# Token-major products that read their tokens as every second place, and residual rows that hold two neighbouring tokens a partition

## The chip, the cores and the metric

One Trainium2 chip, of which the kernel uses one core. The metric is device time in microseconds (us) of one execution: three runs of the kernel before gave 1893.33, 1895.21 and 1895.46 us, median 1895.21. Everything is fp32: a large product is made as three products of fp32r operands (high parts by high parts, high by low, low by high).

## The reference

Two blocks are applied to 256 tokens of width 2048. The second one also sees 16 meta tokens.

```python
# first block
h = x
h = h + mixer_block(rms_norm(h, norm_mix_w[l]), w_in[l], ...)   # ends in: merged @ w_out
u = rms_norm(h, norm_mlp_w[l])
h = h + jnp.square(jax.nn.relu(u @ w_up[l])) @ w_down[l]        # 2048 -> 8192 -> 2048
x = rms_norm(h, norm_final_w)
# second block
h = jnp.concatenate([meta, x], axis=1)
proj = rmsnorm(h, pre_norm_g) @ w_in_2                          # then two kinds of attention: ya, yb
y = jnp.concatenate([ya, yb], axis=-1) @ w_out_2
h = h + rmsnorm(y, post_norm_g)
return h[:, N_META:, :]
```

## The kernel before

**Weights.** All weights stream through a ring of four slots, in chunks of 256 rows by 512 columns (512 KB). SyncE (SP) issues the transfer into `raw`, ScalarE (ACT) rounds it into `whi`, VectorE (DVE) makes the rest `wlo = raw - whi`, and TensorE (PE) multiplies. A chunk holds two tiles of 128 rows of the contraction (`CK = 2`). Eight chunks (`NC`) make a group, which yields 512 columns of a product.

**Two forms of product.** `chunk_t` takes the weights as the stationary operand and streams the 256 tokens past them: 24 matmuls of 128x256 a chunk, and the result has features on the partitions. `chunk_n` (the natural product) takes 128 tokens as the stationary operand and streams the 512 weight columns: 12 matmuls of 128x512 a chunk, and the result has tokens on the partitions. Its stationary operand is `v[:, kt, toks]`, a run of 128 neighbouring fp32 places in a tile that holds features on the partitions and 256 tokens along each of them; `t` is 0 or 1 for the two halves of the tokens.

**Where the natural product is used.** In the first projection for groups 4, 5, 12 and 13 (`natural`), and in the three stages that add to the residual: `w_out` of the first block (4 groups), `w_down` (4 quarters of 4 groups) and `w_out_2` (4 groups). The residual `h` is a tile of 128 partitions by 2 rows (t) by 2048. It is loaded from `x` by one transfer (line 395) once the attention scores of the first block are issued, and first used when the first group of `w_out` is added to it. The result leaves in five stores (line 423) at the end.

**Turning the rows.** `turn_group` (line 476) transposes 4 feature tiles of both rows of `h` on PE with the identity, 8 transposes a call, into one PSUM tile `turned` of 256 tokens: places 0 to 127 for t = 0 and 128 to 255 for t = 1. It is called four times after `w_out` and four times after the last `w_down`. Line 853 multiplies a matrix of ones by the diagonal of the row scales, which puts the 256 scales along the free axis in the same order (two matmuls).

**Order.** The order of the work on each engine is written out by hand, and the engines meet on semaphores. PE's order is: the first projection (22 groups, with the matmuls of the chunked scan and of attention put between chunks), the branch products, `w_out`, four quarters of `w_up` and `w_down`, the second projection (13 groups, with the second block's attention between chunks), `w_out_2`. In the scan, `level_scores` (line 548) has k_both as its stationary operand and reads `qp` for its moving operand in runs of 1, 2, 4, ... 64 neighbouring elements at levels 1 to 7, from two places in turn.

Of the kernel before, what the change touches and what calls it, by code (L numbers as in the profile page):

```python
# [15 lines left out]
P = 128  # L16
D = 2048
T = 256
NT = T // P
# [15 lines left out]
CK = 2  # L35
NC = KT // CK
# [75 lines left out]
def program(nc, x, w_in, lb_logits, hg_norm_w, rel_bias, w_branch_a, w_branch_b, w_out, norm_mix_w,  # L112
# [3 lines left out]
    with ExitStack() as ctx:  # L116
# [18 lines left out]
        ones = sb("ones", [P, P])  # L135
# [221 lines left out]
        def turned(n, i):  # L357

            o = (i % 2) * T
            return ps[:, 4 + 2 * (n % 2) + i // 2, o:o + T]  # L360
# [4 lines left out]
        @block.sync  # L365
        def _(sp):
            def chunk(c0, k, src):

                if not isinstance(c0, int) or c0 + k >= SLOTS:
                    sp.wait_ge(wlo_ready, c0 + k - SLOTS + 1)  # L370
                    sp.sem_inc(sp_turn, 1)
                sp.dma_start(raw[:, k % SLOTS], src).then_inc(raw_in[k % SLOTS], 16)

            def rows(w, k, cols):
                return w[:, CK * k:CK * k + CK, cols]

            sp.dma_start(ident[:], identity).then_inc(ident_in, 16)
            sp.dma_start(mix_rows[:], norm_mix_w[0].rearrange("(k p) -> k p", p=P)).then_inc(mix_in, 16)
            for c in range(4):
                cols = slice(c * CW, (c + 1) * CW)  # L380
                sp.dma_start(x_nat[:, :, cols], x[0, :, cols].rearrange("(t p) d -> p t d", p=P)).then_inc(x_in[c], 16)
                if c == 0:
                    first = rows(w_in_t, 0, slice(0, CW))
                    sp.dma_start(raw[:, 0, 0], first[:, 0]).then_inc(half_in, 16)
                    sp.dma_start(raw[:, 0, 1], first[:, 1]).then_inc(raw_in[0], 16)
                else:
                    chunk(C_IN, c, rows(w_in_t, c, slice(0, CW)))
            for k in range(4, NC):
                chunk(C_IN, k, rows(w_in_t, k, slice(0, CW)))
            with sp.Fori(1, G_IN) as g:  # L390
                for k in range(NC):
                    chunk(C_IN + NC * g, k, rows(w_in_t, k, bass.ds(g * CW, CW)))

            sp.wait_ge(at_s, AH)
            sp.dma_start(h[:], x[0].rearrange("(t p) d -> p t d", p=P)).then_inc(h_in, 16)
            with sp.Fori(0, 4) as n:
                for k in range(NC):
                    w = w_a_t if k < NC // 2 else w_b_t
                    chunk(C_BR + NC * n, k, rows(w, k % (NC // 2), bass.ds(n * CW, CW)))
            with sp.Fori(0, 4) as n:  # L400
                for k in range(NC):
                    chunk(C_OUT + NC * n, k, rows(w_out_t, k, bass.ds(n * CW, CW)))
            with sp.Fori(0, QUARTERS) as q:
                with sp.Fori(0, 4) as n:
                    for k in range(NC):
                        chunk(C_FF + 8 * NC * q + NC * n, k, rows(w_up_t, k, bass.ds(q * D + n * CW, CW)))
                with sp.Fori(0, 4) as n:
                    for k in range(NC):
                        chunk(C_FF + 8 * NC * q + 4 * NC + NC * n, k,
                              w_down_t[:, bass.ds(q * KT + CK * k, CK), bass.ds(n * CW, CW)])  # L410
            for j, col in enumerate(IN2_COLS):
                for k in range(NC):
                    chunk(C_IN2 + NC * j, k, rows(w_in2_t, k, slice(col, col + CW)))
            with sp.Fori(0, 4) as n:
                for k in range(NC):

                    chunk(C_OUT2 + NC * n, k, rows(w_out2_t, (k + NC // 2) % NC, bass.ds(n * CW, CW)))
            i = 0
            for t in range(NT):
                for lo, hi in OUT_COLS[t]:  # L420
                    i += 1
                    sp.wait_ge(y_out, i)
                    sp.dma_start(out[0, t * P:(t + 1) * P, lo:hi], y2[:, t, lo:hi]).then_inc(stored, 16)
            sp.wait_ge(stored, 16 * i)


# [1 line left out]
        def _(pe):  # L428
# [18 lines left out]
                                     stop=last and j == CK - 1 and i == 2, skip_group_check=True)  # L447
                ins.then_inc(pe_done, 1)

            def chunk_n(c0, k, kt0, xh, xl, s, first, last, halves=range(NT)):  # L450

                pe.wait_ge(wlo_ready, c0 + k + 1)
                for j in range(CK):
                    kt = kt0 + j
                    for t in halves:
                        toks = slice(t * P, (t + 1) * P)
                        for i, (v, w) in enumerate(((xh, whi), (xh, wlo), (xl, whi))):
                            ins = mm(ps[:, 2 * s + t, :], v[:, kt, toks], w[:, k % SLOTS, j, :],  # L458
                                     start=first and j == 0 and i == 0,
                                     stop=last and j == CK - 1 and i == 2, skip_group_check=True)  # L460
                if NT - 1 in halves:
                    ins.then_inc(pe_done, 1)
                return ins
# [4 lines left out]
            def turn_group(b, n, freed):  # L468

                pe.wait_ge(set_free[n % 2], freed)  # L470
                if n >= 2:
                    pe.wait_ge(x_ready, KT * b + 4 * n - 4)
                for i in range(4):
                    kt = 4 * n + i
                    for t in range(NT):
                        ins = nc.tensor.transpose(turned(n, i)[:, t * P:(t + 1) * P],  # L476
                                                  h[:, t, kt * P:(kt + 1) * P], ident[:])
                    if i % 2 == 1:
                        ins.then_inc(n_tr, 1)
# [136 lines left out]
            for g in range(G_IN):  # L616
                c0, s = C_IN + NC * g, g % 2
                if g >= 2:
                    pe.wait_ge(set_free[s], g // 2)
                if g == G_LEVEL:  # L620
                    pe.wait_ge(meta_ready, 1)
                natural = g in (4, 5, 12, 13)
                for k in range(NC):
                    if g == 0:
                        if k == 0:
                            warm(11)
                            turn_start(0)
                            warm(9)
                        if k < 3:
                            turn_start(k + 1)  # L630
                        if k == 3:
                            turn_vectors()
                        if k == 6:
                            row_scale()
                        pe.wait_ge(x_ready, CK * (k + 1))
                    if natural:
                        chunk_n(c0, k, CK * k, uhi, ulo, s, k == 0, k == NC - 1)
                    else:
                        chunk_t(c0, k, CK * k, uhi, ulo, blocks(s), T, k == 0, k == NC - 1)
                    if k == 0 and g == 2:  # L640
                        turn_meta()
                    if k == 1 and G_LEVEL <= g < G_HGOUT:
                        level_scores(g - G_LEVEL)
                    if k == 1 and g == G_HGOUT:
                        hg_output()
                    if k == 7 and g == G_HGOUT:
                        hg_squares()
                    if k == 2 and g == G_HGOUT + 1:
                        pe.wait_ge(hg_sd, 4)
                        shift_phase(4, lambda i: acc[:, i, :])  # L650
                    at = NC * (g - G_ATT) + k
                    for part, late in ((att_values, 5), (att_turn, 4), (att_scores, 0)):
                        if pair_at(at - late) is not None:
                            part(pair_at(at - late))
                    if at == PAIR_STEP * (AH // 2):
                        shift_phase(5, lambda i: prob[:, 0, i * P:(i + 1) * P])
# [171 lines left out]
            for j in range(G_IN2):  # L828
# [15 lines left out]
                for k in range(NC):  # L844
                    if j == 0:
                        if k == 2:
                            turn_group(2, 3, down_free[3])
                        pe.wait_ge(x_ready, 2 * KT + CK * (k + 1))
                        if k == NC - 1:
                            pe.wait_ge(r_diag, NT)  # L850
                            pe.wait_ge(x_ready, 3 * KT)
                            for t in range(NT):
                                ins = mm(ps[:, 6, t * P:(t + 1) * P], ones[:], diag[:, t, :], start=True, stop=True)
                            ins.then_inc(r_mm, 1)
                    if j == 5:
                        pe.wait_ge(hi_packed, CK * k + CK - 1)
# [1191 lines left out]
```

## Time and profile before

| what | value |
|---|---|
| runs | 1893.33, 1895.21, 1895.46 us; median 1895.21 |
| profiled execution | span 1893.3 us, which is the time of the lowest run; nothing lies around the span |
| PE busy | 1879.6 us (99%) |
| PEld (weight loads) busy | 1743.7 us (92%) |
| DVE / ACT / POOL busy | 1101.4 / 889.3 / 143.6 us |
| granted TensorE clock | 0.999 |
| DMA | 346.47 MB, mean 183 GB/s |

PE and PEld are one engine: PEld is the loading of the stationary operand, PE the streaming of the moving one. The time that one matmul takes in a full stream is not the "mean ns of one", since matmuls overlap; it is the length of a stretch over the number of matmuls in it, called the pitch below.

### The profile page before, as it was taken

The page shows a single profiled execution, that of the slowest core. Times are in us where ns is not written, and L with a number is a line of the kernel's source. Part 1 is how long each engine was busy: PE and PEld are TensorE (multiplying, and loading weights), DVE is VectorE, ACT ScalarE, POOL GpSimd, SP SyncE. Part 2 cuts the span into 40 slices and gives each one's busy share as a digit, 9 for nine tenths or more (in the row PEclk, how much of TensorE's full clock was granted, in tenths as well). Part 3 has the DMA queues.
Part 4 walks back from the last instruction along what each step waited for, and adds up shares of the span by engine and source line. Part 5 has one row for each costly group of instructions (what it writes and reads, how often), then busy time and mean ns, then how long its engine had stood idle before and what let it go on. Part 6 is the DMA issues. An engine that isn't in the chain of part 4 may idle for free.

```text
span 1893.3 us, 33876 instructions
## 1 busy us (share of the span) xinstructions
PE 1879.6 (99%) x13432; PEld 1743.7 (92%) x13432; DVE 1101.4 (58%) x1270; ACT 889.3 (47%) x1171; POOL 143.6 (8%) x122
## 2 busy tenths in 40 slices
PE   9999999999999999999999999999999999999998
PEld 9989998999999889988998899899889999899986
DVE  6556766667655555545445445445565556767664
ACT  6544444455544445443444344334454355664543
POOL 2001322411001100000010000000010000000000
PEclk9999999999999999999999999999999999999999
DMA  8566565566565656656665665566556655354454
GB/s 270 184 181 177 181 179 178 165 200 180 168 231 191 214 186 179 194 198 192 196 192 193 194 191 194 194 190 190 189 185 181 179 170 150 105 147 144 156 190 143
DMA packets 176434, 346.47 MB, mean 183 GB/s; under 512 B 10976, under 2 KB 11184, under 8 KB 175776
## 3 DMA queue, kind: packets, MB, share of 16 engines
q1 hardware_dynamic: 174176, 337.76, 57.2%
q0 software_dynamic: 2128, 6.82, 1.4%
q8 instruction: 101, 1.65, 0.4%
q14 instruction: 29, 0.24, 0.0%
HBM read 342.44 MB, written 2.10 MB: 182 GB/s over the span
## 4 chain that ended last, share of the span: by engine, by line
PE 97%; DVE 1%; ACT 0%; DMA 0%; issue 0%; SPq 0%; DVEq 0%; ACTq 0%
PE ps L446 58%; PE ps L458 33%; PE ps L548 1%; PE ps L781 1%; DVE wlo L1301 1%; PE ps L771 1%; PE ps L748 1%; PE ps L791 0%; DMA raw<-in_w_in_dram 0%; ACT whi L899 0%; PE ps L476 0%; PE ps L759 0%; PE ps L599 0%; PE ps L591 0%; DVE xlo L1323 0%; PE ps L610 0%
## 5 line engine op out<-in xcount | busy, mean ns | idle before, releaser
L1301 DVE TENSOR_TENSOR wlo<-raw,whi 128x1024 fp32r<-128x1024 f32 x631 | 796.5, 1268 | 698.1 <-ACT whi L899 697.1
L899 ACT ACTIVATE whi<-raw 128x1024 fp32r<-128x1024 f32 x631 | 664.5, 1058 | 886.3 <-PE ps L446 551.5
L446 PE MATMUL ps<-xhi,whi 128*128 128x256 f32 (+1 forms) x1904 | 542.2, 285 | 0.4 <-DVE wlo L1301 0.3
L446 PE MATMUL ps<-xhi,wlo 128*128 128x256 f32 (+1 forms) x1904 | 531.3, 279 | 0.0
L446 PE MATMUL ps<-xlo,whi 128*128 128x256 f32 x1664 | 462.5, 278 | 0.0
L446 PEld LDWEIGHTS ps<-xhi,whi 128*128 128x128 f32 x1904 | 359.1, 189 | 9.3 <-issue 6.7
L446 PEld LDWEIGHTS ps<-xhi,wlo 128*128 128x128 f32 x1904 | 357.8, 188 | 0.0
L446 PEld LDWEIGHTS ps<-xlo,whi 128*128 128x128 f32 x1664 | 313.4, 188 | 1.5 <-issue 0.7
L446 PE MATMUL ps<-x2hi,whi 128*128 128x256 f32 x1024 | 282.8, 276 | 0.0
L446 PE MATMUL ps<-x2hi,wlo 128*128 128x256 f32 x1024 | 282.7, 276 | 0.0
L446 PE MATMUL ps<-x2lo,whi 128*128 128x256 f32 x1024 | 282.7, 276 | 0.0
L446 PEld LDWEIGHTS ps<-x2lo,whi 128*128 128x128 f32 x1024 | 192.2, 188 | 0.2
L446 PEld LDWEIGHTS ps<-x2hi,whi 128*128 128x128 f32 x1024 | 192.2, 188 | 0.2
L446 PEld LDWEIGHTS ps<-x2hi,wlo 128*128 128x128 f32 x1024 | 192.2, 188 | 0.0
L458 PE MATMUL ps<-whi,ya_lo 128*128 128x512 f32 x256 | 100.8, 394 | 0.0
L458 PE MATMUL ps<-whi,yb_lo 128*128 128x512 f32 x256 | 100.8, 394 | 0.0
L458 PE MATMUL ps<-whi,xlo 128*128 128x512 f32 x256 | 100.8, 394 | 0.0
L458 PE MATMUL ps<-wlo,ya_hi 128*128 128x512 f32 x256 | 100.3, 392 | 0.0
L458 PE MATMUL ps<-wlo,yb_hi 128*128 128x512 f32 x256 | 100.2, 392 | 0.0
L458 PE MATMUL ps<-whi,xhi 128*128 128x512 f32 x256 | 100.2, 391 | 0.0
L458 PE MATMUL ps<-wlo,xhi 128*128 128x512 f32 x256 | 100.1, 391 | 0.0
L458 PE MATMUL ps<-whi,ya_hi 128*128 128x512 f32 x256 | 99.7, 390 | 0.0
(373 smaller groups left out, 2370.6 us busy)
## 6 DMA issues: line engine op xcount, KB each, us to landing
raw<-in_w_in_dram SPq DMA_DIRECT2D x279, 512.0 KB, 3.8
raw<-in_w_up_dram SPq DMA_DIRECT2D x128, 512.0 KB, 3.7
raw<-in_w_down_dram SPq DMA_DIRECT2D x128, 512.0 KB, 3.7
raw<-in_w_out_dram SPq DMA_DIRECT2D x64, 512.0 KB, 3.8
raw<-in_w_branch_a_dram SPq DMA_DIRECT2D x16, 512.0 KB, 4.9
raw<-in_w_branch_b_dram SPq DMA_DIRECT2D x16, 512.0 KB, 3.8
x_nat<-in_x_dram SPq DMA_DIRECT2D x4, 512.0 KB, 7.4
rel<-in_rel_turned_dram POOLq DMA_DIRECT2D x8, 256.0 KB, 4.3
```

Source lines behind the costliest of these rows:

```text
L446: ins = mm(outs[b], w[:, k % SLOTS, j, cols], v, start=start, stop=last and j == CK - 1 and i == 2, skip_group_check=True)
L458: ins = mm(ps[:, 2 * s + t, :], v[:, kt, toks], w[:, k % SLOTS, j, :], start=first and j == 0 and i == 0, stop=last and j == CK - 1 and i ...
L548: ins = mm(misc[:, hd // 4, (hd % 4) * P:(hd % 4 + 1) * P], k_both[:, hd, :], spread(qp[:, hd, 0:1], *both_tiles), start=True, stop=True)
L748: ins = mm(ps[:, 4 + i, 0:TM], qb[f, hd, t * P:(t + 1) * P], kb[f, hd, :], start=True, stop=True)
L771: ins = nc.tensor.transpose(ps[:, 6, i * P:(i + 1) * P], p[:, i * P:(i + 1) * P], ident[:])
L781: ins = mm(ps[:, 7, 0:P], pt2[:, u % 2, i * P:(i + 1) * P], v, start=i == 0, stop=i == 2)
L899: f(whi[:, k % SLOTS], raw[:, k % SLOTS], ACT.Copy).then_inc(whi_ready, 1)
L1301: tt(wlo[:, k % SLOTS], raw[:, k % SLOTS], whi[:, k % SLOTS], ALU.subtract).then_inc(wlo_ready, 1)
```

## The change

The tokens that a partition of the residual holds become neighbours: partition p holds tokens 2p and 2p+1, where it held p and 128+p. So the load of `h` and the stores of the result address the tokens in that way, the transposes and the row of scales write every second place of their PSUM tile, and `chunk_n` takes every second place of 256 as its stationary tokens. The four natural groups of the first projection keep their order (`step=1`).

```diff
             sp.wait_ge(at_s, AH)
-            sp.dma_start(h[:], x[0].rearrange("(t p) d -> p t d", p=P)).then_inc(h_in, 16)
+            sp.dma_start(h[:], x[0].rearrange("(p t) d -> p t d", p=P)).then_inc(h_in, 16)
...
-                    sp.dma_start(out[0, t * P:(t + 1) * P, lo:hi], y2[:, t, lo:hi]).then_inc(stored, 16)
+                    sp.dma_start(out[0].rearrange("(p t) d -> p t d", p=P)[:, t, lo:hi], y2[:, t, lo:hi]).then_inc(stored, 16)
...
-            def chunk_n(c0, k, kt0, xh, xl, s, first, last, halves=range(NT)):
+            def chunk_n(c0, k, kt0, xh, xl, s, first, last, halves=range(NT), step=NT):
...
-                        toks = slice(t * P, (t + 1) * P)
+                        toks = slice(t, NT * P, NT) if step == NT else slice(t * P, (t + 1) * P)
...
-                        ins = nc.tensor.transpose(turned(n, i)[:, t * P:(t + 1) * P],
+                        ins = nc.tensor.transpose(turned(n, i)[:, t:T:NT],
...
-                        chunk_n(c0, k, CK * k, uhi, ulo, s, k == 0, k == NC - 1)
+                        chunk_n(c0, k, CK * k, uhi, ulo, s, k == 0, k == NC - 1, step=1)
...
-                                ins = mm(ps[:, 6, t * P:(t + 1) * P], ones[:], diag[:, t, :], start=True, stop=True)
+                                ins = mm(ps[:, 6, t:T:NT], ones[:], diag[:, t, :], start=True, stop=True)
```

No instruction is added, removed or moved: PE, DVE, ACT and POOL have the same rows in the same order. On SP one row reads otherwise, the load of `h` after the loop over the first projection's weights and before the loop over the branch weights (shapes are partitions by the rest):

```order
@@ -37,5 +37,5 @@
 L390 REGISTER_ALU
 L390 COMPARE_AND_BRANCH
-L395 DMA h<-in_x_dram 128x2x2048
+L395 DMA h<-in_x_dram 128x4096
 L396 UNCONDITIONAL_BRANCH
 L396 ISA
```

What a partition gets from memory was two runs of 2048 elements, and is now one of 4096.

## Rows read from the trace of the kernel before

**Rows 1.** The page: busy time of each engine, granted clock by slice.

```profile
span 1893.3 us, 33876 instructions
PE 1879.6 (99%) x13432; PEld 1743.7 (92%) x13432; DVE 1101.4 (58%) x1270; ACT 889.3 (47%) x1171; POOL 143.6 (8%) x122
PEclk9999999999999999999999999999999999999999
```

**Rows 2.** All waits of PE over the run: us, times, longest.

```profile
PE ps L504 <- DMA mix_rows<-in_norm_mix_w_dram: 2.9, 1, 2.9
PE ps L771 <- DVE p L1752: 0.7, 1, 0.7
PE ps L446 <- DVE wlo L1301: 0.3, 1, 0.3
```

**Rows 3.** Chain in order of time (start, us, what): natural and transposed products.

```profile
300.99 21.99 PE ps L458 x96
...
814.72 87.89 PE ps L458 x384
902.61 87.07 PE ps L446 x768
...
1797.86 87.91 PE ps L458 x384
```

**Rows 4.** Line 458 by operand: duration min/median/max ns, first and last start.

```profile
L458 PEld LDWEIGHTS ps<-whi,xhi x256: 187/188/192, 103.5 to 725.7; 128*128 128x128 f32 x128
...
L458 PEld LDWEIGHTS ps<-whi,yb_lo x256: 187/188/189, 825.8 to 1429.5; 128*128 128x128 f32 x128
L458 PEld LDWEIGHTS ps<-whi,yt_b_hi x64: 187/188/188, 1797.6 to 1873.7; 128*128 128x128 f32 x64
```

**Rows 5.** Timeline in a natural stage (start us, us).

```profile
830.35 0.39 PE L458 MATMUL ps<-whi,yb_hi 128*128 128x512 f32 x1
830.36 0.19 PEld L458 LDWEIGHTS ps<-wlo,yb_hi 128*128 128x128 f32 x1
830.58 0.39 PE L458 MATMUL ps<-wlo,yb_hi 128*128 128x512 f32 x1
```

**Rows 6.** Timeline in a transposed stage.

```profile
939.88 0.28 PE L446 MATMUL ps<-x2hi,whi 128*128 128x256 f32 x1
939.88 0.19 PEld L446 LDWEIGHTS ps<-x2lo,whi 128*128 128x128 f32 x1
939.99 0.28 PE L446 MATMUL ps<-x2lo,whi 128*128 128x256 f32 x1
940.00 0.19 PEld L446 LDWEIGHTS ps<-x2hi,wlo 128*128 128x128 f32 x1
```

**Rows 7.** Chain: line 548 at levels 1, 2, 3 and 6.

```profile
156.77 2.66 PE ps L548 x16
...
181.21 1.92 PE ps L548 x16
...
204.91 1.78 PE ps L548 x16
...
275.59 1.78 PE ps L548 x16
```

**Rows 8.** Chain: transposes between natural chunks, and the row of scales.

```profile
709.40 0.87 PE ps L476 x8
710.27 16.50 PE ps L458 x72
726.77 5.46 PE ps L446 x48
...
1452.24 0.68 PE ps L853 x4
```

**Rows 9.** Transposes of h, the whole run.

```profile
L476 PE MATMUL ps<-ident,h x64: 270/272/273, 663.5 to 1436.7; 128*128 128x128 f32 x64
```

**Rows 10.** Transfers: line, KB each, median us to landing.

```profile
h<-in_x_dram SPq DMA_DIRECT2D x1, 2048.0 KB, 9.6
out_dram<-y SPq DMA_DIRECT2D x3, 512.0 KB, 2.7
...
out_dram<-y SPq DMA_DIRECT2D x2, 256.0 KB, 2.8
```

**Rows 11.** Chain around the load of h, its issue, and its first use.

```profile
530.11 106.09 PE ps L446 x936
...
528.68 0.38 SPq L395 DMA_DIRECT2D h<-in_x_dram  x1
...
L1582 DVE TENSOR_TENSOR h<-h,ps x4: 1210/1212/1216, 660.5 to 729.1; 128x1024 f32<-128x1024 f32 x4
```

## The prediction

> **What bounds the kernel now.** I read the page first: PE is busy for 1879.6 of 1893.3 us, at full clock in every slice [rows 1]. Then the waits of PE: its longest is 2.9 us, at the start, and those inside the run are 0.7 us or less [rows 2]. So the time is the length of PE's own stream, and the change can only act by making PE's instructions longer or shorter, by starving PE, or in the tail after the last matmul. Nothing is moved on any engine, so I look at what each touched instruction costs PE.
>
> The pitch comes from the chain in order of time. A natural stretch of 384 matmuls takes 87.89 us, so 228.9 ns each; a transposed stretch of 768 takes 87.07 us, so 113.4 ns each [rows 3]. It hardly varies: 87.91 us for `w_out_2`, and 21.99 / 96 = 229.1 ns in the first projection. The timeline shows what lies beside what. In a natural stage a load of the stationary operand starts as the matmul before it starts (830.36 against 830.35), and the next matmul comes 0.23 us later [rows 5]. The load's own duration is 188 ns [rows 4], but this isn't the time that it holds the loader: in a transposed stage a load of the same 128x128 shape starts every 0.11 us, beside matmuls of 113.4 ns, and PE doesn't fall back [rows 3, 6]. So a contiguous load needs at most 113.4 ns of loader time, and a natural matmul offers 228.9. The cover is 228.9 - 113.4 = 115.5 ns a load.
>
> **Term 1: the stationary tokens, every second place.** Touched are w_out (4 groups x 8 chunks x 12 = 384 loads), w_down (4 x 384 = 1536) and w_out_2 (384): 2304 loads. No stationary operand in this trace is read with a step, so I bound the cost by the nearest rows, those in which PE reads its moving operand in pieces. Line 548 makes 16 passes of 128 columns a level; only the run length of its moving operand changes. At levels 3 and 6 (runs of 4 and 32) it takes 1.78 us, at level 2 (runs of 2) 1.92 us, at level 1 (single elements, alternating between two far places) 2.66 us [rows 7]. Per pass of 128 elements: 111 ns, +9 ns, +55 ns. With a step of two, 128 elements span 1 KB and no two are adjacent, but unlike level 1 the next one lies only 8 bytes on. If a 16-byte piece is what is fetched, the new read uses two elements of each, as level 2 does. So a load should need 113.4 + 9 = 122 ns, at worst 113.4 + 55 = 168 ns; both are under 228.9. Exposed cost: 0. Without the cover it would be 2304 x 9 ns = 21 us, or 2304 x 55 ns = 127 us.
>
> The Trainium skill (SBUF — State Buffer, Specifications) gives lines of 16 bytes and asks for two hits in each for full bandwidth; by it, fp32 at a step of two reads at full speed, and the term is 0 even without cover. Level 1 against level 3 agrees with the direction of that rule, level 2 with its +9 ns only roughly.
>
> A load is not covered by a natural matmul where a shorter instruction stands before it: at the start of the six natural stretches after transposed ones (113.4 ns matmuls before it), and after six of the eight turn_group calls (8 transposes in 0.87 us, 109 ns each [rows 8]; the other two stand between transposed chunks). Twelve loads at 9 ns are 0.1 us, at 55 ns 0.7 us. I take 0.1.
>
> **Term 2: transposes that write every second place of PSUM.** 64 transposes [rows 9], all on PE's chain at 109 ns. No row has a PSUM write with a step. Lower bound 0: a transposed 128-column pass writes 128 elements in 109 ns, and if they go to PSUM in pairs of 8 bytes, the new form touches 128 pairs in 109 ns, 0.85 ns a pair; a natural matmul already writes 512 adjacent columns in 228.9 ns, so 256 pairs at 0.89 ns a pair. The rate needed is within 5% of one that is sustained. Upper bound from the nearest row: +55 ns, the price of single elements on the read side [rows 7], which is 64 x 55 = 3.5 us. I take +9 ns, nearer to the first since the rate argument speaks for it: 64 x 9 = 0.6 us.
>
> **Term 3: the row of scales.** Four passes in 0.68 us, once [rows 8]: 4 x 9 = 0.04 us, at most 4 x 55 = 0.2 us.
>
> **Term 4: the load of h.** It is issued at 528.68, lands 9.6 us later, and is first used at 660.5 [rows 10, 11]; 120 us cover it. Behind it on SP stand the first branch chunks, and while they come PE runs 936 matmuls without a break from 530.11 [rows 11]. One run of 16 KB a partition instead of two of 8 KB moves the same bytes. If it landed a few us later, PE has up to four chunks of 2.7 us (24 x 113.4 ns) in hand. 0 either way.
>
> **Term 5: the stores.** Same bytes, same rows of 2 or 4 KB, now 16 KB apart in memory instead of 8 KB. Only the last is in the tail; the five land in 2.6 to 2.8 us [rows 10]. I take 0, with 0.2 us either way.
>
> **Sum.** 0 + 0.1 + 0.6 + 0.04 + 0 + 0 = +0.7 us on a span of 1893.3, so 1894.0. The profiled execution is the lowest of the three runs, and the median lies 1.9 us above it: 1895.9 us. By the upper bounds of the terms it would be 0.7 + 3.5 + 0.2 + 0.2 = +4.6 us, so about 1900.
>
> **The rivals.**
>
> *A: writes with a step into PSUM are dear* (slower). If each of the 68 passes doubled, the price is 109 ns x 64 + 170 ns x 4 = 7.7 us, so 1902.9. It decides from about 56 ns a pass (3.8 us / 68). For it: nothing in the trace shows such a write. Against it: the rate of pairs above. The Trainium skill (PSUM — Partial Sum Buffer, Specifications) has lines of 8 bytes and says that any non-contiguous pattern slows matmuls significantly, with no figure; by its words this is the outcome to expect, and this trace can neither confirm nor refute it. Chance 0.10.
>
> *B: loads with a step are not free* (slower). Two ways. The loader needs more than 228.9 ns, so more than twice its present time: each ns past that costs 2.3 us, a load of 250 ns makes +49 us, one of four times 113.4 ns +519 us. Or the load disturbs the reading of the moving operand beside it: at level 2's +9 ns a matmul, 2304 x 9 = 21 us, so about 1916. Against the second: counted in 16-byte pieces, a natural matmul now reads 128 moving and will read 64 stationary ones in 228.9 ns, 0.84 a ns; a transposed matmul already reads 64 + 32 in 113.4 ns, 0.85 a ns, without loss. Against the first: even level 1 adds only half of a pass. For both: no row has such a load. It decides from 1.6 ns a matmul (3.8 / 2304). Chance 0.14.
>
> *C: faster.* The pitch is not at its floor: 512 columns take 228.9 ns while two times 256 take 226.8 in the transposed stages. If spreading the load made the natural matmul run at that rate, 2304 x 2.1 = 4.8 us come back: about 1891. For it: the difference is there and steady. Against it: nothing says that the load causes it. Chance 0.05.
>
> *D: no change that can be measured* is the forecast: chance 0.71.
>
> **How the numbers follow.** A difference under 0.2% (3.8 us) can't be told from none. D lies inside (1891.4 to 1899.0), A and B outside above, C just outside below: faster 0.05, same 0.71, slower 0.24. The range takes in D, A (1902.9) and C (about 1891): 1890 to 1904. It leaves out B, 0.14.
>
> **What would show it.** Right: natural stretches of 384 still take 87.9 us, with loads every 0.23 us (the load's own duration may grow from 188 ns without harm); 8 transposes take 0.87 to 0.95 us; waits of PE as before. A shows as groups of 8 transposes of 1.3 us or more with everything else the same. B shows as stretches of 384 above 88.5 us, and above all in a contrast: the natural groups of the first projection, which keep contiguous tokens, stay at 229 ns while w_out, w_down and w_out_2 rise. C shows as the same contrast downward, 87.1 us. Terms 4 and 5 would show as a wait of ACT for a branch chunk that reaches PE, and as a longer landing of the last store. The prediction would be wrong if reading with a step costs more on the loader than on the moving side, from which I took its price.

## The result and the profile after

The changed kernel takes 1918.8 us (median of four runs, 1917.58 to 1919.66) against 1894.27 us for the kernel before: a ratio of 1.0126, interval 1.0112 to 1.0140. It is slower by 24.5 us, outside the range of the prediction (1890 to 1904).

The page of the changed kernel, busy time and clock:

```profile
span 1916.6 us, 33876 instructions
PE 1903.1 (99%) x13432; PEld 1773.6 (93%) x13432; DVE 1101.2 (57%) x1270; ACT 889.3 (46%) x1171; POOL 143.4 (7%) x122
PEclk9999999999999999999999999999999999999999
```

PE gained 23.5 us of busy time with the same instruction count, the same clock, and DVE, ACT and POOL as before [rows 1]. The span grew by 23.3 us. The chain in order of time says where (start us, us, what):

```profile
300.16 21.99 PE ps L458 x96
...
529.28 106.10 PE ps L446 x936
635.38 28.00 PE ps L458 x120
...
727.61 5.65 PE ps L446 x48
733.26 0.87 PE ps L476 x8
734.13 84.80 PE ps L446 x720
818.94 89.59 PE ps L458 x384
908.53 90.45 PE ps L446 x768
```

Up to 635 us nothing has changed: the contiguous natural groups of the first projection still take 21.99 us per 96 [rows 3], and the branch stage 106.10 us [rows 11]. From the first stepped load on, a natural stretch of 384 takes 89.6 us instead of 87.89, and, which I had not looked for, a stretch of 768 transposed matmuls takes 90.45 instead of 87.07 [rows 3]. Not one instruction of that second kind was changed. In pitch: 233.3 instead of 228.9 ns and 117.8 instead of 113.4 ns, 4.4 ns more in both, whatever the number of columns. The sum closes: 2304 stepped matmuls x 4.4 = 10.1 us, and 4 up stages x 768 x 4.4 = 13.5 us, together 23.6 us; the span grew by 23.3, with a start that was 0.8 us shorter and a stretch from the row of scales to `w_out_2` that was 0.5 us longer.

The durations of the matmuls show the same two levels. Line 446, the up stage between 909 and 998 us of the changed kernel, then the kernel before in 903 to 989 us (duration ns min/median/max):

```profile
L446 PE MATMUL ps<-x2lo,whi x253: 281/281/282, 908.8 to 997.9; 128*128 128x256 f32 x127
```

```profile
L446 PE MATMUL ps<-x2lo,whi x254: 276/276/281, 902.9 to 989.0; 128*128 128x256 f32 x127
```

And the stepped loads themselves (line 458, changed kernel), against 187 to 188 ns in [rows 4], with the transposes of h below, as in [rows 9]:

```profile
L458 PEld LDWEIGHTS ps<-whi,yb_hi x256: 194/194/198, 829.7 to 1450.2; 128*128 128x128 f32 x128
...
L476 PE MATMUL ps<-ident,h x64: 270/272/273, 663.2 to 1457.8; 128*128 128x128 f32 x64
```

The slow level was already in the trace of the kernel before, in a place that I passed over: its chain has a transposed stretch at the start with 31.09 / 264 = 117.8 ns, and its matmuls there last 281 ns.

```profile
30.57 31.09 PE ps L446 x264
```

I call such a steady pitch of a stream its rhythm. So the kernel before has two rhythms for one and the same kind of stream, a fast one of 113.4 ns and a slow one of 117.8 ns. The question is what a stepped load has to do with them.

### The profile page after: what moved, and what is told of

Same layout as the page of the kernel before. It is cut to its first block, busy times and chain, and to the rows that moved or that the text cites. A ratio compares the mean times of both kernels' runs of the same rounds, so it can differ in the third digit from the quotient of the medians.

```text
span 1916.6 us, 33876 instructions
## 1 busy us (share of the span) xinstructions
PE 1903.1 (99%) x13432; PEld 1773.6 (93%) x13432; DVE 1101.2 (57%) x1270; ACT 889.3 (46%) x1171; POOL 143.4 (7%) x122
## 4 chain that ended last, share of the span: by engine, by line
PE 97%; DVE 1%; ACT 0%; DMA 0%; issue 0%; SPq 0%; DVEq 0%; ACTq 0%
PE ps L446 58%; PE ps L458 33%; PE ps L548 1%; PE ps L781 1%; DVE wlo L1301 1%; PE ps L771 1%; PE ps L748 1%; PE ps L791 0%; ACT whi L899 0%; PE ps L476 0%; DMA raw<-in_w_in_dram 0%; PE ps L759 0%; PE ps L599 0%; PE ps L591 0%; DVE xlo L1323 0%; PE ps L610 0%
## 5 line engine op out<-in xcount | busy, mean ns | idle before, releaser
L446 PE MATMUL ps<-x2hi,whi 128*128 128x256 f32 x1024 | 287.8, 281 | 0.0
L446 PE MATMUL ps<-x2hi,wlo 128*128 128x256 f32 x1024 | 287.8, 281 | 0.0
L446 PE MATMUL ps<-x2lo,whi 128*128 128x256 f32 x1024 | 287.8, 281 | 0.0
L458 PE MATMUL ps<-whi,yb_hi 128*128 128x512 f32 x256 | 101.2, 396 | 0.0
```

The source lines that it names most:

```text
L446: ins = mm(outs[b], w[:, k % SLOTS, j, cols], v, start=start, stop=last and j == CK - 1 and i == 2, skip_group_check=True)
```

## The experiments

**Which part of the change costs.** `e1_contig`: the three calls of `chunk_n` in the residual stages get `step=1`; all else of the change stays.

```diff
-                    chunk_n(C_OUT + NC * n, k, CK * k, uhi, ulo, n % 2, k == 0, k == NC - 1)
+                    chunk_n(C_OUT + NC * n, k, CK * k, uhi, ulo, n % 2, k == 0, k == NC - 1, step=1)
```

> The changed kernel with contiguous stationary tokens in all natural products; the new load of h, the stores, the transposes and the row of scales with a step stay. It leaves out the matching order of the tokens, so rows of the residual and of the products belong to different tokens. Theory S (the stepped loads alone cause the loss, in their own stages and in the up stages between them): back to the kernel before within 0.2%, natural pitch 228.9 ns, up stages 113.4 ns, and the 64 transposes as before. Rival W (writes with a step into PSUM, or the new layout of h, slow the up stages): natural stages at 228.9 ns, up stages stay at 117.8 ns, so about +13.5 us against before.

Measured: ratio to the kernel before 1.0002 (0.9993 to 1.0012). The chain has the rows of before:

```profile
812.78 87.89 PE ps L458 x384
900.67 87.07 PE ps L446 x768
```

Theory S holds, rival W is out. The stepped loads alone set off the loss of 24 us; the writes with a step into PSUM, the load of h and the stores cost nothing that can be measured.

**Price of each load, or a state.** `e2_wout_only`: as e1, but `w_out` keeps its stepped loads.

> The changed kernel with the stepped loads kept in w_out (384 loads) and contiguous ones in w_down and w_out_2; so the tokens of those two products are paired with the wrong rows. Theory R (a stepped load moves PE's stream into a slower rhythm, which lasts when the loads are contiguous again, until something else breaks it): the up stages stay at 117.8 ns and w_down is slow too, so +15 to +24 us against before. Rival L (the price lies on each stepped load and its neighbour only): w_out at 233.3 ns, everything after it as before, so +1.7 us, which is no measurable difference.

Measured: 1.0038 (1.0024 to 1.0052), 1900.7 against 1893.53 us.

```profile
712.43 16.80 PE ps L458 x72
...
735.76 84.80 PE ps L446 x720
820.56 89.60 PE ps L458 x384
910.16 87.06 PE ps L446 x768
```

Only the natural matmuls up to 729 us have stepped loads. The up stage behind them runs at 84.80 / 720 = 117.8 ns, and then the first w_down stage, whose loads are contiguous, at 89.60 / 384 = 233.3 ns. So contiguous loads have the slow rhythm too, and it is handed on. Then it ends, at the start of the next up stage, with nothing put in. Of theory R the core holds (a state that outlives the loads), while "+15 to +24 us" was wrong: it outlives the stepped loads by two stages. Slow are 384 + 768 + 384 = 1536 matmuls, x 4.4 ns = 6.8 us, and 7.2 us were measured. Rival L is out.

The two slow streams of 512 columns have the same pitch but aren't the same inside. The contiguous loads here last 189 ns, beside matmuls of 397 to 398 ns; the stepped ones of the changed kernel last 194 ns, beside matmuls of 392 to 398 ns. So the step lengthens the load itself, and it isn't shown that both streams are in one and the same state.

The trace shows one thing more. Two stretches of the first projection, where nothing differs from the kernel before for PE, are slow in this execution; in the trace of before they take 41.02 and 27.47 us.

```profile
62.46 42.60 PE ps L446 x360
105.06 28.00 PE ps L458 x120
```

The trace of `e11` below has the same two slow, and the stretch of 264 takes 31.09 us in some traces and 29.94 in others. So the rhythm of a stretch can differ between executions of the same instructions. A time from one run can be off by 2 us for this alone, and what a single trace shows behind a break may be chance.

**The slow rhythm without any stepped load.** `e5_before_noshift`: the kernel before without the three dead transposes (transposes whose result nobody reads; `shift_phase`, line 509) that it runs at the end of the first projection.

```diff
-                    if at == PAIR_STEP * (AH // 2):
-                        shift_phase(5, lambda i: prob[:, 0, i * P:(i + 1) * P])
```

> The kernel before without the three transposes that it runs at the end of the first projection (a dead computation; results unchanged). Before them its transposed products ran at 117.8 ns, after them at 113.3 ns. Theory R: the branch stage stays at 117.8 ns, and perhaps all up to the second projection: contiguous natural loads then show whether they have a slow rhythm too (233 ns) or return by themselves to 228.9 ns. Up to +3.4 us for the branch stage alone (768 x 4.4 ns), up to +27 us if it lasts. Rivals L and W: no change but -0.3 us.

Measured: 1.0028 (1.0018 to 1.0037), 1898.47 against 1893.53 us, so removing work made it slower.

```profile
528.23 110.44 PE ps L446 x936
638.67 28.00 PE ps L458 x120
666.67 0.87 PE ps L476 x8
667.55 21.99 PE ps L458 x96
```

The branch stage takes 110.44 us instead of 106.09 [rows 11], the contiguous natural loads behind it start at 28.00 / 120 = 233.3 ns, and the eight transposes of `turn_group` end it: 21.99 / 96 = 229.1 ns. In the changed kernel the same eight transposes end nothing, neither between stepped natural matmuls (22.41 us for 96 behind them) nor in the first up stage, where all loads are contiguous: 117.8 ns before them and 84.80 / 720 = 117.8 ns behind. So stepped loads bring the slow rhythm back, and eight transposes don't end it in every stream of contiguous loads either.

**Can the stepped stream be fast at all.** `e6_shift_in_down` puts 1, 2, ... 12 transposes into the twelve w_down groups of three quarters.

```diff
+                        if k == 3 and not last:
+                            for i in range(1 + g + 4 * q):
+                                nc.tensor.transpose(ps[:, 4, 0:P], ident[:], ident[:])
```

> The changed kernel with 1, 2, 3, ... 12 transposes of the identity put after the fourth chunk of the twelve w_down groups of the first three quarters, one more in each next group (results unchanged). Read is the pitch of the 48 natural matmuls behind each piece. Theory R1 (the stepped loads only happen to enter in the slow rhythm; there is a fast one for them too): behind some of the counts the pitch falls from 233.3 to 228.9 ns. Theory R2 (a stream of stepped loads has only the slow rhythm): 233.3 ns behind all twelve. In both the span grows by the 78 transposes, some 8 us against the changed kernel.

Measured: 1925.62 us in one run. Two of the twelve breaks, those of 2 and of 11 transposes, with the stretches behind them:

```profile
852.00 0.22 PE ps L700 x2
852.22 22.40 PE ps L458 x96
...
1240.43 1.20 PE ps L700 x11
1241.63 22.40 PE ps L458 x96
```

Behind all twelve counts the stretches take 22.40 or 22.41 us for 96 matmuls, or 11.20 or 11.21 us for 48: 233.3 to 233.5 ns. Theory R2: for a stream in which all loads are stepped I found only the slow rhythm. `e7_first_stepped` (stepped loads in the four natural groups of the first projection as well) says the same in another place.

> The changed kernel with stepped loads also in the four natural groups of the first projection (384 more loads; the values of that projection get their tokens in the wrong order). Two of the groups are entered from a fast transposed stage, and other matmuls stand between their chunks. Theory R2: 233.3 ns in all four groups, and the transposed chunks behind them slow (117.8 ns) until something else stands between. Theory R1: some pieces at 228.9 ns. Against the changed kernel +1.7 us for the loads themselves, and up to +6 us where the levels of the scan, which run between transposed stretches of 192, do not reset it.

Measured: 1919.28 us in one run; the 1.7 us expected against the changed kernel's 1918.8 is less than the 2 us over which that kernel's own runs spread.

```profile
134.47 16.81 PE ps L458 x72
151.27 5.66 PE ps L446 x48
156.93 2.66 PE ps L548 x16
159.59 21.78 PE ps L446 x192
...
353.26 16.96 PE ps L446 x144
```

233.4 ns in the natural groups, 117.9 ns in the 48 transposed matmuls behind them, and 113.4 ns again as soon as the 16 passes of line 548 have stood between. Behind the later two groups the other work of the scan (48 short passes in 5.4 us) ends nothing: the 144 transposed matmuls after it take 16.96 us, 117.8 ns each, where the changed kernel has 16.34.

**One load in three.** `e8_one_of_three`: in w_down only one of the three products has a stepped load, another in each quarter, none in the last.

```diff
+                            stepped = step == NT and only in (None, i)
+                            toks = slice(t, NT * P, NT) if stepped else slice(t * P, (t + 1) * P)
```

> The changed kernel with contiguous loads in w_out and w_out_2, and in w_down stepped ones for one of the three products only: high by high in quarter 0, high by low in quarter 1, low by high in quarter 2, none in quarter 3 (tokens are mixed between the parts of a product). Theory R2 in its strict form (each stepped load is what can't be followed at the fast rhythm): 230.4 ns (a third of the 4.4) in the three quarters. Rhythm as a property of the whole stream: either 228.9 or 233.3 ns in each, nothing between, and the up stage behind a slow one slow as well. Quarter 3 is 228.9 ns unless it inherits a slow rhythm.

Measured: 1903.95 us in one run.

```profile
813.97 88.78 PE ps L459 x384
902.75 87.05 PE ps L446 x768
989.80 88.77 PE ps L459 x384
1078.57 90.46 PE ps L446 x768
```

88.77 / 384 = 231.2 ns: a third value, half of the 4.4 up, which neither expectation had. It is steady from end to end of a stretch (starts 226, 236 and 232 ns apart in turn), so it isn't a mixture of fast and slow pieces. It is the same whichever of the three products has the stepped load. Only the stepped loads are longer, 194 ns beside 187 or 188 for the other two. In the last quarter, where no load is stepped, the natural stage first inherits the slow rhythm (28.00 us for 120), and the eight transposes of `turn_group` end it (21.99 us for 96), as in e5. Behind it the up stage is fast once and slow twice: whether a slow piece hands its rhythm on isn't decided by that piece alone.

**Repairing what is handed on.** `e4_shift_up`: three transposes after the seventh chunk of each up stage.

```diff
+                        if g == 0 and k == 6:
+                            shift_phase(4, lambda i: ident[:])
```

> The changed kernel with three transposes of the identity put after the seventh chunk of each of the four up stages (results unchanged), as the kernel does elsewhere. Theory R: if a short piece of other work can reset the rhythm, the rest of each up stage runs at 113.4 ns: about 600 of 768 matmuls x 4 x 4.4 ns = -10.6 us, +1.3 us for the transposes, so about -9 us against the changed kernel. If three transposes do not reset it, +1.3 us. Rival L and rival W: +1.3 us, up stages at 117.8 ns throughout.

Measured: 1907.75 us, 1.0076 (1.0059 to 1.0093), 11 us below the changed kernel's 1918.8.

```profile
905.59 19.79 PE ps L446 x168
925.38 0.33 PE ps L509 x3
925.70 68.02 PE ps L446 x600
993.72 89.60 PE ps L458 x384
```

117.8 ns, three transposes in 0.33 us, 113.4 ns, and then the natural stage has its 233.3 again. The other three quarters read alike. `e9_counts_up` asks for the count (1, 2, 4 and 5 in the four quarters, twice each).

> The changed kernel with transposes of the identity after the seventh chunk of the first and of the third group of each up stage: 1 in quarter 0, 2 in quarter 1, 4 in quarter 2, 5 in quarter 3 (results unchanged). Three of them brought the transposed stream from 117.8 to 113.4 ns. If the break in the stream as such resets it, all four counts do, and the second piece changes nothing. If the count matters, some leave it at 117.8 ns, and a second piece may flip it either way.

Measured: 1913.5 us in one run.

```profile
746.48 0.11 PE ps L692
746.59 45.23 PE ps L446 x384
...
906.98 19.05 PE ps L446 x168
926.02 0.22 PE ps L692 x2
926.25 45.23 PE ps L446 x384
...
1106.95 43.54 PE ps L446 x384
```

One transpose leaves the stage slow (45.23 / 384 = 117.8). In the second quarter the stage happened to start fast (19.05 / 168 = 113.4), and two transposes made it slow. Four make it fast (117.8 ns before, 43.54 / 384 = 113.4 behind), and so do five; a second piece of the same count changes nothing in any quarter. This is one execution, so each count is seen in two places only; that three and four transposes work every time rests on the times of e4 and e12, four and six runs. `e12_repair` uses four, as early as the buffers allow.

> The changed kernel with four transposes of the identity as early as possible in each up stage: after the seventh chunk in quarter 0, after the first chunk in the others (results unchanged). Four left the fast rhythm behind them wherever they were tried. Of 4 x 768 transposed matmuls about 600 + 3 x 744 = 2832 go from 117.8 to 113.4 ns: -12.6 us, +1.8 us for the transposes, so about -11 us against the changed kernel, +13 us against the kernel before. The 2304 stepped loads stay at 233.3 ns.

Measured: 1906.55 us, 1.0067 (1.0055 to 1.0079).

```profile
908.33 0.44 PE ps L692 x4
908.77 84.34 PE ps L446 x744
```

That is 12 us back; the 2304 stepped loads keep their part, 10 us, and the transposes cost 1.8. `e3_out2_only` shows this part by itself, with no stage behind it to hand on to.

> The changed kernel with stepped loads in w_out_2 only (the tokens of w_out and w_down are paired with the wrong rows). No stage follows it. The stepped loads' own price: 384 x 4.4 ns = +1.7 us, pitch 233.3 ns in the last 384 matmuls, 228.9 and 113.4 ns in all before.

Measured: 1895.11 us in one run beside 1893.6 of the kernel before. The difference is within the spread of single runs, and it is the pitch that answers: 89.61 us for the last 384, the rest of the residual stages as before:

```profile
1796.20 89.61 PE ps L458 x384
```

**Is there something to gain in the kernel before.** `e10_before_resets` puts three transposes into two of its own slow stretches, `e11_wide_resets` three, four and five into the stage of 272 columns.

> The kernel before with three transposes of the identity at two places where its transposed stream runs at 117.8 ns: after the first chunk of group 1 (some 216 matmuls of the stretch of 264 follow) and after the seventh chunk of the sixteenth group (results unchanged). If they reset it: 113.4 ns behind them, about -1 + 0.3 us and -0.2 + 0.3 us, which no timing can tell; the pitch is what is read. The place after hg_squares, where the kernel's own three transposes left 117.8 ns behind them, says that they may not.

Measured: 1894.23 us in one run beside 1893.6. In the first place there was nothing to reset: in this execution the stretch was fast (8.18 us for 72) before the transposes came; in the second the kernel's own three left it slow, and three more, 96 matmuls later, made it fast:

```profile
379.22 0.33 PE ps L509 x3
379.55 11.31 PE ps L446 x96
390.86 0.33 PE ps L509 x3
391.19 5.46 PE ps L446 x48
```

> The kernel before with 3, 4 and 5 transposes of the identity after the sixth chunk of groups 1, 2 and 3 of the second projection, whose 272-column matmuls run at 123.33 ns (results unchanged). If 123.33 ns is the slow of two rhythms for this length, the pitch falls behind one of the counts, to 119 or 120 ns, and up to 3 us come back; if it is the only one, +1.3 us and the same pitch.

Measured: 1896.95 us in one run. 23.69 / 192 = 123.4 ns behind three and, to the same hundredth, behind four; all the pieces with those around the five add up to 103.4 us for the 840 matmuls, as in the kernel before. I found no faster rhythm for that length.

```profile
1474.45 23.69 PE ps L446 x192
```

No version here beats the kernel before. Most of what it loses to the slow rhythm lies in seven stretches of 96 in its attention stage (0.4 us each), and a break of three transposes costs 0.33 us; the stretches of 264 and 144 lose 1.2 and 0.6 us more in the execution profiled.

## Why the prediction was wrong

**The bound and the way to look** were right: PE's stream is the time, and nothing else moved. Waits of PE, the tail (1916.6 - 1909.1 = 7.5 us behind the last matmul) and the other engines are as before.

**Term 1 failed**, at "Exposed cost: 0". I asked whether the longer load fits under the matmul. It does: the load grew from 188 to 194 ns, and there were 115 ns of cover. But the pitch of a stream of loads and matmuls isn't only the longer of the two. The stream has rhythms 4.4 ns apart, and when all its loads are stepped the fast one wasn't reached in any trace; what sets them is not shown. The term measured 2304 x 4.4 = 10.1 us instead of 0.1. Rival B's second way came nearest (a load that fits under its matmul and still slows the stream), priced at 9 ns where it was 4.4; that it does so by disturbing the reading of the moving operand, as I wrote there, no run shows. I had argued it down by counting 16-byte pieces; that count leaves out the larger part of the loss, since the up stages ran fast and slow with the same operands. Nor was it the way to be wrong that I named last, a step dearer on the loader than on the moving side: the load grew by 6 ns, less than the 9 I took from there. The Trainium skill (TensorE: Matmul & The Clock Gate, step-by-step part) has loads and moving reads on two ports, so that a load doesn't take bandwidth from the matmul that runs. The trace can't tell whether bandwidth is taken; the changed kernel against e1 shows that the load's pattern alone lengthens the pitch.

**A term was missing**: 13.5 us in the up stages, more than half of the loss. Neither the sum nor a rival had it, because I costed only touched instructions. I also wrote that the pitch "hardly varies" after reading three natural stretches and one transposed; the row of 264 matmuls at 117.8 ns stood in the same view. It would have shown that the pitch has two values, and that something other than the instruction chooses between them. The kernel's own helper, three dead transposes with the name `shift_phase`, pointed at it too; e5 measures that its call at the end of the first projection is worth 5 us.

**Terms 2 to 5 were right**: eight transposes take 0.87 us with the step as without, the stores land in 2.7 us as before, h lands in 9.5 us, and e1 puts all of them together at 1.0002. I had 0.6 us for terms 2 and 3, and no difference shows. Rival A is out with them. The Trainium skill (PSUM — Partial Sum Buffer, Specifications) says that a non-contiguous pattern there slows matmuls significantly; for fp32 transposes of 128 columns, one place in two, this trace disagrees: 272 ns before and after. The result is what the argument from the rate of pairs gave; that the writes go in pairs is not shown.

**Rival C** (faster) was out. The contrast that I had named for rival B (first projection unchanged, residual stages up) did show, and its limit of 88.5 us was passed with 89.6.

**What stays open** is why there are two rhythms and what decides which one a stretch takes. A single stepped load in three gives a value between them, the slow one is handed on in most cases and not in all (after slow w_down stages: slow in the changed kernel, fast in e2 and once in e9), the same transposes reset it in one place and not in another, and a stretch can be fast in one execution and slow in the next. The experiments show that the state exists, that streams in which all loads are stepped were at its pitch in every trace, and that a break of three to five transposes ended it in every up stage that was slow, where one and eight did not; they don't show its cause.

## What to carry to other kernels

Where PE is the bound, read the pitch of every stretch of like matmuls (time over count in the chain), not of a few: two values for the same instruction mean that the stream has a state, and then a change can cost in stages that it doesn't touch. Hiding a longer weight load under a longer matmul is not enough to make it free; a stationary operand read at every second fp32 place cost 4.4 ns on each of 2304 matmuls here and as much on the 3072 of the up stages between and behind them. Since the rhythm can differ between executions, take a single trace behind a change as one draw. Put such a step on the side that was free in this case, the writes of transposes into PSUM, and keep stationary reads contiguous.

## What the runs showed of the hardware

- A stream of load and matmul pairs with contiguous operands ran in one of two rhythms at full clock (0.999 granted): 113.4 or 117.8 ns at 256 columns, 228.9 or 233.3 at 512. The difference is 4.4 ns at both lengths. At 272 columns only 123.4 was seen.
- The same stretch was fast in one execution and slow in another: 41.02 us in the kernel before, 42.60 in e2 and e11, for the same 360 matmuls of the first projection.
- The slow rhythm outlived the stepped loads by 1152 matmuls (e2), across a change from 256 to 512 columns. Three dead transposes (0.33 us) ended it for 600 matmuls (e4), eight did not in the first up stage of the changed kernel, and removing three made a kernel slower by 5 us (e5).
- With stepped stationary fp32r operands only 233.3 ns (within 0.2) was seen, behind twelve different breaks (e6) too. With one in three it was 231.2 ns (e8). The stepped load itself lasted 194 ns, a contiguous one beside 512 columns 188, or 189 in the slow rhythm (e2).
- Transposes that write fp32 to every second place of PSUM cost the same as contiguous ones, 0.87 us for eight.
